# Latent attention with two sets of score banks: a head's eight score units in one stretch, then the preceding head's values in one stretch

## The reference, cut to what matters

```python
def attend(qn, qr, kn, kr, v):
    s = (jnp.einsum("bqhd,bkhd->bhqk", qn, kn)
         + jnp.einsum("bqhd,bkd->bhqk", qr, kr)).astype(F32) * scale
    p = jax.nn.softmax(s, axis=-1).astype(v.dtype)
    return jnp.einsum("bhqk,bkhd->bqhd", p, v)
...
ox = lax.map(lambda qq: attend(qq[0], qq[1], kn_all, kr_all, v_all), (to_blocks(qnx), to_blocks(qrx)))
...
yx = (ox * jax.nn.silu(gx)) @ w_out
```

## Time and profile before

| | us |
|---|---|
| median of 3 runs | 3771.32 |
| lowest and highest run | 3769.86, 3773.07 |
| the profiled execution's own time | 3774.33 |
| its span (first to last instruction) | 3772.5 |
| PE busy | 3504.2 (93%) |
| DVE busy | 1869.5 (50%) |
| ACT busy | 1152.1 (31%) |
| POOL busy | 872.1 (23%) |

### The profile page before, as it was taken

The page is one execution under the profiler, slowest core; times in us unless marked ns, Lnnn a source line. Parts: engine busy times, 40 slices in busy tenths (PEclk is TensorE's granted clock), DMA queues, the critical chain, the costliest instruction groups (busy, mean ns, idle before and its releaser), DMA issues. The chain is left out here.

```text
span 3772.5 us, 64563 instructions
## 1 busy us (share of the span) xinstructions
PE 3504.2 (93%) x27290; PEld 2012.5 (53%) x27290; DVE 1869.5 (50%) x2911; ACT 1152.1 (31%) x2214; POOL 872.1 (23%) x544
## 2 busy tenths in 40 slices
PE   8999999999988999999899998998899896887898
PEld 3448864445545666644446446544443334887543
DVE  3336652323217888732456318322758873655322
ACT  1127751112224445411321108212313342221124
POOL 0000013430000000043233210233115761333532
PEclk9999999999999999999999999999999998999999
DMA  6000013325243444430431102110155444533400
GB/s 245 23 23 2 2 68 112 102 76 146 79 130 100 112 108 122 149 118 18 156 106 56 34 0 91 67 45 13 72 221 195 161 157 121 162 109 86 163 12 39
DMA packets 312102, 358.42 MB, mean 95 GB/s; under 512 B 161541, under 2 KB 215029, under 8 KB 309127
## 3 DMA queue, kind: packets, MB, share of 16 engines
q1 hardware_dynamic: 311816, 354.30, 29.1%
HBM read 255.88 MB, written 98.29 MB: 94 GB/s over the span
## 5 line engine op out<-in xcount | busy, mean ns | idle before, releaser
L2197 DVE TENSOR_SCALAR_CACHE_REDUCE la_s<-psum 128x1280 f32<-128x1280 f32 x128 | 191.0, 1492 | 96.6 <-PE psum L2233 96.6
L2166 ACT ACTIVATE la_s<-la_s,la_negm 128x1280 f32<-128x1280 f32 x128 | 175.6, 1372 | 194.3 <-DVE la_s L2197 194.3
L970 POOL TENSOR_TENSOR lg_seven_s<-other_columns 128x512 f32<-128x512 f32 x4 | 5.1, 1264 | 799.2 <-POOLq L112 778.7
L991 PE MATMUL psum<-room,x_rows 128*128 128x512 f32 x320 | 146.7, 602 | 4.8 <-POOL x_rows L970 4.8
L970 POOL TENSOR_TENSOR wg_seven_s<-other_columns 128x512 f32<-128x512 f32 x5 | 6.3, 1267 | 591.8 <-POOLq L112 543.3
L835 DVE CUSTOM_DVE_ANT_0 wa_s<-psum,window_mask_rows 128x640 f32<-128x640 f32 (+1 forms) x128 | 100.6, 786 | 71.5 <-PE psum L890 71.5
L991 PE MATMUL psum<-room,rp_seven_s 128*128 128x512 f32 x256 | 116.9, 600 | 5.4 <-DVE rp_seven_p L1040 5.4
L3313 POOL TENSOR_TENSOR x_rows<-x_rows,pg_g 128x512 f32<-128x512 f32 x56 | 84.0, 1500 | 153.6 <-DVE pg_g L3462 139.8
L793 ACT ACTIVATE wa_s<-wa_s,wa_negm 128x640 f32<-128x640 f32 (+2 forms) x160 | 117.3, 742 | 0.9 <-DVE wa_negm L838 0.9
L991 PE MATMUL psum<-rp_t,rp_seven_s 128*128 128x512 f32 x256 | 116.5, 598 | 0.0
L991 PEld LDWEIGHTS psum<-room,x_rows 128*128 128x128 f32 x320 | 60.9, 194 | 77.5 <-issue 77.5
(11 more groups left out here) (719 smaller groups left out, 7924.9 us busy)
## 6 DMA issues: line engine op xcount, KB each, us to landing
la_v<-latent_v SPq DMA_DIRECT2D x64, 320.0 KB, 5.8
x_rows<-rwkv_raw SPq DMA_DIRECT2D x40, 512.0 KB, 4.7
room<-rwkv_raw SPq DMA_DIRECT2D x33, 512.0 KB, 4.9
later_slot<-in_ada_w_dram SPq DMA_DIRECT2D x16, 1024.0 KB
rwkv_raw<-x_rows SPq DMA_DIRECT2D x64, 256.0 KB, 2.9
rwkv_raw<-x_rows SPq DMA_DIRECT2D x32, 512.0 KB, 3.9
room<-in_odd_w_in_dram SPq DMA_DIRECT2D x6, 2048.0 KB, 13.1
room<-in_even_w_in_dram SPq DMA_DIRECT2D x5, 2048.0 KB, 12.8
```

The source lines that it names most:

```text
L991: last = pe.matmul(bank, left[:, k, :], right[:, k, :], start=fresh and k == 0, stop=k == HK - 1, skip_group_check=True)
L2166: act.activation(s, s, ACT.Exp, scale=-1.0, bias=negm[:, u % RING:u % RING + 1], accum_out=total[:, head(u) % 2, tile(u):tile(u) + 1]).the ...
L2197: dve.tensor_scalar(by_lane(s_sb[:, u % RING, :]), by_lane(s_banks)[:, :, 0:SPAN], -SCALE, FAR, ALU.mult, ALU.min, accum_out=negm[:, u % R ...
```

## The change

- The eight banks become two sets of four. Unit t of head h writes its scores into set (h + t) mod 2, so neighbouring units alternate. The values of head h go into set (h + 1) mod 2, its turn back into one bank, the first of that set, which serve other work at other times. A score unit from the third on waits for the read of the unit two before it (a head's first one for all reads), the second unit of a head also for the evacuation of the head before last, and the first one for its normalising.
- PE's order: a head's eight score units, then 20 blocks of the preceding head's values, the turn back of the head before that, and the other 20 blocks.
- DVE's order: eight reads, eight transposes, one inversion. `la_s` gets eight slots.
- ACT's order: eight exps, normalise two heads back, evacuate the preceding head.
- The even heads' value buffer moves into `first_weights`; only the odd heads' stays in `la_v`. So `first.load` now stands behind the wait for 15 heads' values.

The diff, cut to its core (semaphore lines of `values` and `scores` as they stand now):

```diff
-    NOPE_BLOCKS, KEY_BLOCKS, RING = B_NOPE // LANES, K // LANES, 4
+    NOPE_BLOCKS, KEY_BLOCKS, RING = B_NOPE // LANES, K // LANES, QT
+    SPLIT = KEY_BLOCKS // 2
+    scores_side = lambda u: (u // QT + u % QT) % 2
+    values_side = lambda h: (h + 1) % 2
+    back_side = lambda h: (h + 1) % 2
...
-        k_other, v = sb("k", [P, NOPE_BLOCKS, SPAN]), sb("v", [P, 2, KEY_BLOCKS, B_V])
+        k_other, v = sb("k", [P, NOPE_BLOCKS, SPAN]), [first["v"], sb("v", [P, KEY_BLOCKS, B_V])[:, :, :]]
...
-        s_banks, o_banks = core.banks(0, LANE_GROUPS), core.banks(4, LANE_GROUPS)
+        banks_of = lambda side: core.banks(side * LANE_GROUPS, LANE_GROUPS)
...
+        sums_of = lambda h, r: core.banks(values_side(h) * LANE_GROUPS + r)[:, 0:BANK // 2]
+        back_of = lambda h, t: core.banks(back_side(h) * LANE_GROUPS)[:, t * B_V:(t + 1) * B_V]
...
+                for h in range(H + 2):
+                    if h < H:
+                        for t in range(QT):
+                            exp(h * QT + t)
+                    if h >= 2:
+                        normalise(h - 2)
+                    if 1 <= h <= H:
                         evacuate(h - 1)
...
                 def read_scores(u):
                     dve.wait_ge(s_made, u + 1)
+                    if u >= RING:
+                        dve.wait_ge(turned, u - RING + 1)
...
-                read_scores(0)
-                for u in range(1, UNITS):
-                    read_scores(u)
-                    turn(u - 1)
-                turn(UNITS - 1)
+                for h in range(H):
+                    for t in range(QT):
+                        read_scores(h * QT + t)
+                    for t in range(QT):
+                        turn(h * QT + t)
+                    invert(h)
...
-                    if u:
                         pe.wait_ge(s_read, u)
+                        if h >= 3:
+                            pe.wait_ge(back_read, (h - 2) * QT)
+                    elif t:
+                        if u >= 2:
+                            pe.wait_ge(s_read, u - 1)
+                        if t == 1 and h >= 2:
+                            pe.wait_ge(oT_moved, (h - 1) * LANE_GROUPS)
...
+                def values(h, blocks):
+                    if blocks.start == 0:
+                        pe.wait_ge(s_read, min((h + 1) * QT + QT - 1, UNITS))
                         pe.wait_ge(turned, (h + 1) * QT)
                         pe.wait_ge(v_in[h % 2], (h // 2 + 1) * V_LOADS * 16)
...
                 def turn_back(h):
                     pe.wait_ge(oT_moved, (h + 1) * LANE_GROUPS)
...
+                    pe.wait_ge(s_read, min((h + 3) * QT, UNITS))
...
+                for h in range(H + 1):
+                    if h < H:
+                        for t in range(QT):
+                            scores(h * QT + t)
+                    if h:
+                        values(h - 1, range(0, SPLIT))
+                    if h >= 2:
+                        turn_back(h - 2)
+                    if h:
+                        values(h - 1, range(SPLIT, KEY_BLOCKS))
+                turn_back(H - 1)
...
+                      "v": row(room[:, :, :])[:, (1 + NOPE_BLOCKS) * SPAN:(1 + NOPE_BLOCKS) * SPAN + B_KEYS // LANES * B_V].rearrange("p (b d) -> p b d", d=B_V),
...
+                sp.wait_ge(o_made, heads)
                 first.load(sp)
-                sp.wait_ge(o_made, heads)
```

More of the change, by code:

```diff
@@ L2173, in evacuate @@
                     for r in range(LANE_GROUPS):
-                        act.activation(oT[:, :, lanes(r)], core.banks(4 + r)[:, 0:BANK // 2].rearrange("p (t q) -> p t q", t=QT), ACT.Copy).then_inc(oT_moved, 1)
+                        act.activation(oT[:, :, lanes(r)], sums_of(h, r).rearrange("p (t q) -> p t q", t=QT), ACT.Copy).then_inc(oT_moved, 1)
                 def normalise(h):
@@ L2179, in normalise @@
                     for t in range(QT):
[L2180 to L2184, removed]
-                        evacuate(h - 1)
[L2186 to L2191, removed]
+                        act.activation(o[:, t, h * B_V:(h + 1) * B_V], back_of(h, t), ACT.Copy, scale=inverse[:, h % 2, t:t + 1]).then_inc(back_read, 1)
+                for h in range(H + 2):
[5 more added lines that the diff above has]
+                    if 1 <= h <= H:
+                        evacuate(h - 1)
             @block.vector
@@ L2220, in scores @@
                 def scores(u):
-                    h, g = head(u), u // HALF
+                    h, t, g = head(u), tile(u), u // HALF
                     queries = slice((u % HALF) * P, (u % HALF + 1) * P)
@@ L2224, in scores @@
                         pe.wait_ge(q_in[g % 2], (g + 1) // 2 * Q_LOADS * 16)
-                    if h and tile(u) == 0:
+                    if h and t == 0:
                         pe.wait_ge(k_in[h % 2], (h + 1) // 2 * K_LOADS * 16)
-                    if u:
                         pe.wait_ge(s_read, u)
+                        if h >= 3:
[5 more added lines that the diff above has]
+                            pe.wait_ge(oT_moved, (h - 1) * LANE_GROUPS)
                     for b in range(NOPE_BLOCKS + 1):
@@ L2253, in turn_back @@
                         pe.wait_ge(halves_made, 1)
+                    pe.wait_ge(s_read, min((h + 3) * QT, UNITS))
                     for t in range(QT):
-                        last = pe.matmul(back_of(t), oT[:, t, :], both_halves[:, :], start=True, stop=True)
+                        last = pe.matmul(back_of(h, t), oT[:, t, :], both_halves[:, :], start=True, stop=True)
                     last.then_inc(back_made, 1)
[L2258 to L2266, removed]
+                for h in range(H + 1):
[4 more added lines that the diff above has]
+                        values(h - 1, range(0, SPLIT))
+                    if h >= 2:
+                        turn_back(h - 2)
+                    if h:
+                        values(h - 1, range(SPLIT, KEY_BLOCKS))
+                turn_back(H - 1)
 class StickStart:
```

28 lines of the change are left out of this document (11 added, 17 removed).

## The result

| | us |
|---|---|
| before, median of 4 runs on the same chip | 3770.59 (3769.33 to 3773.07) |
| changed, median of 4 runs | 3713.85 (3706.17 to 3714.24) |
| ratio, 95% interval | 0.9837 (0.9823 to 0.985) |
| the profiled execution of the changed kernel, its span | 3713.88, 3712.1 |

Two identical repeats on other chips gave 0.9863 (0.9836 to 0.989) and 0.983 (0.9817 to 0.9844). The forecast was 3716, faster.

A forecast was written before the change was run, and what follows sets the result against it. The prediction took a PE-DVE loop through one set of four banks, 3.52 us a unit, as the bound. Gains of 40.5 (heads), 8.7 (beginning), 8.3 (end) and -2 (loads) sum to 55.5 us: median 3716, range 3698 to 3746.

The forecast's parts named there:

- The heads: 13 repeated attention heads: two bank sets let two score units share one 3.52 us loop; 28.9 to 25.8 a head, gain 40.5 us.
- I keep the 0.5 us of stops: 25.8: Repeated heads: stops that no engine caused were assumed to remain, 0.5 us on top of 25.3 a head.
- the bound of 25.2 a head: Repeated heads: the forecast's fast limit for one head, 25.2 us, giving a gain of 48 us over 13 heads.
- The beginning: Stage's first matmul to the third head's first read: 67.0 us before, gain 8.7 (about -6 to +12).
- I charge head 1 2.5 us for a low clock: Beginning, second head: PE stands some 8 us while DVE transposes, so 2.5 us were added for a low clock.
- The end: Last head's first read to last normalised tile: 52.6 us before, 44.3 forecast, gain 8.3 (5 to 10.8).
- so I add 2.5: End: after PE's wait of some 2.5 us for transposes a low clock was feared; 2.5 us added to 41.8.
- The loads moved back: Stage's end: next stage's loads wait for head 14's values, so its own first load queues behind; -2 us (0 to -6).
- PE starved of instructions: Rival, value stretches: 320 value matmuls in one stretch bring a 2.07 us stop a head; 27 us, 3743; chance 0.12.
- The clock falls in every head: Rival, repeated heads: PE's pause nears 1.93 us, four slow score units cost 6.2 a head; 3796 us; chance 0.04.
- The sum: Whole program: 40.5 + 8.7 + 8.3 - 2 = 55.5 us gained, median 3716.

## Why the prediction was right, and where its terms were off

**The heads** were right in mechanism and nearly in size. PE's head was forecast as 25.13 and is 25.10. DVE was forecast 0.18 late and is 0.22 early: its head by itself is 24.88, read off where PE was relieved. The step of a transpose was 1.43 in the forecast and is 1.41 (eight in 11.26), and the first read follows 0.08 after the reciprocal starts, where 0.16 was counted. The sentence that failed is "I keep the 0.5 us of stops: 25.8". The list of the heads shows no stop in 11 of 13 (before, five of 13 were longer than the rest). So 13 heads gave 48.0 and not 40.5, the bound of 25.2 a head. Why the stops went with the old order is not shown. In the repeats one or two heads took 25.3 to 25.7, so a few small ones may come.

**The beginning** gained 12.8 for 8.7. Unit 1 was read 2.47 us after unit 0, not 3.3, since the clock came back inside that unit; this and DVE's steps put the second head's first read 29.4 us after the stage's first matmul instead of 30.6. The step that failed is "I charge head 1 2.5 us for a low clock". The low clock was there (first unit 2.52 for 16 matmuls, as in the earlier trace rows), but under DVE's transposes: the second head took 24.88, DVE's own length. What the forecast also lacked is the queue: PE's wait of 7.95 there ended with the queries, not with DVE. It cost nothing, as the run with the queries first shows.

**The end** gained 6.0 for 8.3. The step that failed is "so I add 2.5" for the clock, and the wait under it: PE was to wait some 2.5 us for the transposes and waited 1.28, and the clock was 1.00 through the values. The mechanism itself was sound, as the kernel with less PE work shows. There PE waited 3.11 us at this place, and the values then ran slow at first (the row, and a window of it with the clock at 0.51):

```profile
1522.79 6.26 PE L2257 MATMUL psum<-la_pT,la_v 32*64 32x256 f32 x160 [3.11 <-issue]
```

```profile
1523.00:1526.00 3.00, 3.00 (x65) 2.70 (x61) 0.00 (x0) 0.00 (x0) 0.00 (x0) 0.51 1.04 383
```

In the changed kernel two stops of 2.84 and 1.36 beside the transfers stood in the clock's place, the kind that the earlier trace rows had shown once; the sum had no term for them. With the loads behind the values the end is 42.2, where the forecast before that addition was 41.8.

**The loads moved back** cost nothing that can be seen at the next stage's start: the next stage's first matmul did not wait for its weights, and DVE's wait for `lg_b` is 1.82, it was 1.79. The -2 was not needed there. (The stops of the end came beside these loads, as said.)

**The rivals.** Stops like those of "PE starved of instructions" came, but only at the end, beside the transfers; that instructions were missing is not shown. In the 13 heads, with the DMA at 0.49, no such stop stood. "The clock falls in every head" happened once. In the third head PE waited 1.91 us for DVE, and the next unit ran slow:

```profile
1174.24 1.94 PE L2244 MATMUL psum<-first_weights,columns 32*128 32x320 f32 x16 [1.91 <-DVE la_s L2200]
```

That head took 26.58. In a repeat, where the same wait was 1.29, the unit ran at full pace (1.36) and the head took 25.05. The mechanism is as forecast, but it cost 1.5 us in that head, where the rival had four slow units and 6.2. What keeps it out of the others is that DVE is early there, not late. And in the kernel with less PE work, where PE waits 1.52 us for DVE in a head, the next unit ran at full pace all the same (1.36), as did the units behind pauses of 1.62 us in the run that waits for every read.

**The sum.** The stage gave 66.8 us for 55.5, and the total was near because the rest of the program gave back 6.4 in this profile. By the medians the gain is 56.7. The forecast of 3716 is therefore right in sign and mechanism; that it is so close in size is luck, as its terms are off by 2 to 8 us.

## What to carry to other kernels

Where two engines wait for each other through one buffer, each well short of busy, find the loop and its period first; with a second buffer each engine's period is the sum of its own list, and the larger sum is the new bound. Order both lists to fit it: with PE's new order, the second set of banks without the reads in a row lost 21 us against before, the reads in a row without the overlap of two sets lost 150. When the two sums come out within 1% of each other, taking work off the larger gives no more than their difference, here 0.22 us a head, and off the smaller nothing.

## What was not expected

- Beside transfers of some 400 GB/s (396 to 403 in the windows of the stops) PE stood 2.84 us with no engine to wait for, at the same matmul in six profiles, and did not in four others with loads under way. By what the transfers hold PE up, and when, is not shown.
- The same stop does not always cost the clock. After it the changed kernel's next 52 matmuls took 1.94 us, at a granted clock of 1.00; in the repeat on the second chip they took 3.42, at 0.56. The stretch of the latter in windows, and its row:

```profile
1529.50:1533.00 3.50, 3.42 (x53) 2.59 (x52) 0.00 (x0) 0.00 (x0) 0.00 (x0) 0.56 1.20 487
```

```profile
1529.58 3.42 PE L2257 MATMUL psum<-la_pT,la_v 32*64 32x256 f32 x52 [2.84 <-issue]
```

- Eight transposes that last 1.51 us each when they stand alone take 11.26 together in a row, 1.41 a piece: each starts before the one ahead has ended.
